# Products on x times the norm's weights for the first token group: one decoder step on one core

## The chip, the core and the metric

The kernel runs on one core of one Trainium2 chip. The metric is the device time of one execution in microseconds (us); 2378.42 is the median of three runs of the kernel before.

## What is computed

One layer of a hybrid decoder over 1088 tokens (1024 of a prompt, 64 of eight samples), width 1024, in fp32. The change touches only its first stage, the first half-step FFN, with d_ff = 2816:

```python
def rmsnorm(x, g):
    xf = xf * lax.rsqrt(jnp.mean(xf * xf, axis=-1, keepdims=True) + EPS)
    return xf.astype(x.dtype) * g
def swiglu_ffn(x, g, w_gate, w_up, w_down):
    h = rmsnorm(x, g)
    return (jax.nn.silu(h @ w_gate) * (h @ w_up)) @ w_down
x = x + 0.5 * swiglu_ffn(x, p['ffn1_norm'], ...)
```

The root of a token multiplies its whole column, so it can be applied to x or to the product. Token mixing, cross attention, a second FFN and a last norm follow.

## The kernel before, in words

Activations lie as 128 partitions by 8 rows (`KT`, 1024 features) by tokens. The tokens are three groups n = 0, 1, 2 of 384, 384 and 320 (`NS`). Every fp32 product is made of three (`split_mm`, L1782 to L1784): a weight tile and its operand are each split into a high part in fp32r (a copy) and a low part (the rest), and TensorE makes high by high, high by low and low by high.

The FFN runs in 11 iterations (`ITS`) of two of the 22 tiles of d_ff. An iteration has six `gate_up` steps and then 24 down tiles. In iteration 0 the steps go group by group (`ffn_step`): steps 0 and 1 are group 0 with the first and second tile, steps 2 and 3 group 1, steps 4 and 5 group 2. A step is 24 gate products and 24 up products, into PSUM banks 4 and 5 (even steps) or 6 and 7 (odd). Down tile (n, m) is six products into bank m % 4, and from the fifth tile on it waits until VectorE has added an earlier tile into x (`x_added`, L1342).

Each engine works off its own list in order:

- SyncE issues the loads: x for group 0 in two halves of 768 KB, gate and up weights of the first tile (512 KB each), x of group 1, weights, x of group 2, weights, and then `st_raw`.
- ScalarE copies the weights' high parts (`ffn_prep`, L783), squares x (`norm_squares`, L818), takes the root (`norm_root`, L843), copies the high parts of normed rows (`pair_highs`, L858), applies silu (`step`, L869), and copies the high part of the later stages' weights (`stage_prep`, L794).
- GpSimd makes the low parts of weights: `low` (L704) and `stage_low` (L709), in the order in which ScalarE delivers.
- VectorE adds up the squares (`norm_sum`, L1173 and L1174), takes the reciprocal (L1166), scales the rows by weight and root (`pair_scale`, L1244), makes their low part (`pair_low`, L1256), and in `hidden(s)` makes silu times up (`hf`, L1326), its high part (`h_hi`, L1330) and low part (`h_lo`, L1332). After all six `hidden` it adds the down tiles into x.
- TensorE also makes the norm's statistics (`norm_stats`, L1809) and spreads a root over the partitions (`norm_spread`, L1844) into a bank called `rb`. In ffn1 of group 0 all of this stands ahead of the first product: squares, sums, statistics, root, spread, rows, highs, lows.

Pairs of rows (`PAIRED`) are released one by one: a product of rows 2i and 2i + 1 waits for `normed`, the i-th low part.

## Time and profile before

| | |
|---|---|
| median of 3 runs | 2378.42 us (2377.48 to 2379.25) |
| profiled execution | 2381.26 us |
| its span | 2379.5 us |
| TensorE busy | 2345.2 us (99%) |
| VectorE / ScalarE / GpSimd busy | 1065.7 / 500.7 / 519.7 us |
| granted TensorE clock, mean | 0.995 |

The table gives averages over the whole span. TensorE is busy nearly throughout; a query of a stretch of the timeline shows when an engine works and what ended its idle time.

### The profile page before, as it was taken

Reading aid. Unit: us, or ns where it says so; the run is one execution under the profiler, and the core shown is the slowest. Engines: PE = TensorE matmul, PEld = TensorE weight load, DVE = VectorE, ACT = ScalarE, POOL = GpSimd, SP = SyncE. Lnnn points to the kernel's source line nnn. Section 1 sums busy time; section 2 is a strip of 40 time slices with the busy share of each in tenths; the row PEclk is TensorE's granted clock in tenths of the full one; section 3 lists DMA queues with packets and bytes.
Section 4 is the critical chain, followed back from the end, with each engine's and each line's share of the span. In section 5 each row is a group of like instructions: output and inputs, shape, how many; then the busy total and the mean of one; then the engine's idle time right before and its main releaser. Section 6 shows DMA issues by size and latency. Waiting matters only on the chain. (4 is left out here: it accounts for less than half of the span.)

```text
span 2379.5 us, 36667 instructions
## 1 busy us (share of the span) xinstructions
PE 2345.2 (99%) x15002; PEld 2286.1 (96%) x15002; DVE 1065.7 (45%) x1696; ACT 500.7 (21%) x705; POOL 519.7 (22%) x239
## 2 busy tenths in 40 slices
PE   7999999999999999999999999999999999999998
PEld 7999999999999989899889999799999999999998
DVE  6534334444334574565642423445443344443345
ACT  4222212122211241321410211331111111111112
POOL 2444334344432000000001000022221222221121
PEclk9999999999999999999989999999999999999999
DMA  4554444454452465566668476731111011101112
GB/s 158 213 212 167 159 194 174 152 212 167 159 194 89 154 217 181 212 222 240 231 240 327 142 265 237 276 124 54 51 38 52 36 53 35 53 35 53 35 36 76
DMA packets 89475, 352.50 MB, mean 148 GB/s; under 512 B 8944, under 2 KB 16432, under 8 KB 79152
## 3 DMA queue, kind: packets, MB, share of 16 engines
q1 hardware_dynamic: 89104, 351.12, 40.1%
q8 instruction: 64, 1.05, 0.2%
q10 hardware_dynamic: 288, 0.18, 0.0%
q14 instruction: 19, 0.16, 0.0%
HBM read 280.54 MB, written 70.72 MB: 148 GB/s over the span
## 5 line engine op out<-in xcount | busy, mean ns | idle before, releaser
L1782 PE MATMUL ps<-a_hi,w_sb 128*128 128x384 f32 (+1 forms) x2112 | 690.9, 327 | 6.6 <-DVE a_lo L1256 4.5
L1784 PE MATMUL ps<-a_hi,w_sb 128*128 128x384 f32 (+1 forms) x2112 | 689.1, 326 | 0.0
L1783 PE MATMUL ps<-a_lo,w_sb 128*128 128x384 f32 (+1 forms) x2112 | 689.0, 326 | 0.0
L704 POOL TENSOR_TENSOR w_sb<-w_raw,w_sb 128x1024 fp32r<-128x1024 f32 x132 | 318.0, 2418 | 1063.7 <-ACT w_sb L783 1063.7
L1782 PEld LDWEIGHTS ps<-a_hi,w_sb 128*128 128x128 f32 x2112 | 396.9, 188 | 8.4 <-issue 3.6
L1783 PEld LDWEIGHTS ps<-a_lo,w_sb 128*128 128x128 f32 x2112 | 397.0, 188 | 0.0
L1784 PEld LDWEIGHTS ps<-a_hi,w_sb 128*128 128x128 f32 x2112 | 397.0, 188 | 0.0
L1342 DVE SCALAR_TENSOR_TENSOR x<-ps,x 128x384 f32<-128x384 f32 (+1 forms) x528 | 279.2, 534 | 202.2 <-PE ps L1784 202.1
L1326 DVE TENSOR_TENSOR hf<-sil,ps 128x384 f32<-128x384 f32 x132 | 70.2, 532 | 635.3 <-ACT sil L869 635.3
L1782 PE MATMUL ps<-h_hi,w_sb 128*128 128x384 f32 (+1 forms) x1056 | 344.6, 326 | 0.3 <-DVE h_lo L1332 0.2
L1784 PE MATMUL ps<-h_hi,w_sb 128*128 128x384 f32 (+1 forms) x1056 | 344.2, 326 | 0.0
L1783 PE MATMUL ps<-h_lo,w_sb 128*128 128x384 f32 (+1 forms) x1056 | 344.1, 326 | 0.0
L869 ACT ACTIVATE sil<-ps 128x384 f32<-128x384 f32 x132 | 62.6, 474 | 1123.8 <-PE ps L1784 1123.8
L1332 DVE TENSOR_TENSOR h_lo<-hf,h_hi 128x384 fp32r<-128x384 f32 x132 | 241.6, 1830 | 4.6
L1782 PEld LDWEIGHTS ps<-h_hi,w_sb 128*128 128x128 f32 x1056 | 198.2, 188 | 1.0 <-DVE h_lo L1332 0.5
L1783 PEld LDWEIGHTS ps<-h_lo,w_sb 128*128 128x128 f32 x1056 | 198.2, 188 | 0.0
L1784 PEld LDWEIGHTS ps<-h_hi,w_sb 128*128 128x128 f32 x1056 | 198.2, 188 | 0.0
L738 POOL TENSOR_TENSOR sq<-sq 128x768 f32<-128x768 f32 (+2 forms) x17 | 30.0, 1763 | 648.0 <-ACT sq L818 648.0
L783 ACT ACTIVATE w_sb<-w_raw 128x1024 fp32r<-128x1024 f32 x132 | 139.1, 1055 | 98.5 <-DMA w_raw<-in_ffn_gate 90.4
L709 POOL TENSOR_TENSOR st_w<-st_raw,st_w 128x1024 fp32r<-128x1024 f32 x60 | 145.4, 2454 | 48.7 <-ACT st_w L794 48.7
L1782 PE MATMUL ps<-mo_hi,w_sb 128*128 128x384 f32 (+1 forms) x384 | 125.7, 327 | 0.6 <-DVE mo_lo L1726 0.6
L1784 PE MATMUL ps<-mo_hi,w_sb 128*128 128x384 f32 (+1 forms) x384 | 125.1, 326 | 0.0
(266 smaller groups left out, 2731.7 us busy)
## 6 DMA issues: line engine op xcount, KB each, us to landing
w_sb<-split SPq DMA_DIRECT2D x148, 1024.0 KB, 5.3
split<-st_w SPq DMA_DIRECT2D x60, 1024.0 KB, 4.1
st_raw<-in_mix_tiles SPq DMA_DIRECT2D x60, 512.0 KB, 5.8
w_raw<-in_ffn_gate SPq DMA_DIRECT2D x44, 512.0 KB, 3.6
w_raw<-in_ffn_up SPq DMA_DIRECT2D x44, 512.0 KB, 4.4
w_raw<-in_ffn_down SPq DMA_DIRECT2D x44, 512.0 KB, 4.3
kc<-in_cache_k SPq DMA_DIRECT2D x5, 1024.0 KB, 9.2
kc<-in_cache_v SPq DMA_DIRECT2D x4, 1024.0 KB, 9.8
```

Of the source, the lines that this page charges most:

```text
L704: nc.gpsimd.tensor_tensor(w_lo_sb[:, slot_, :], raw[:, slot_, :], w_hi_sb[:, slot_, :].bitcast(F32), ALU.subtract)\
L709: nc.gpsimd.tensor_tensor(st_w[:, j % 3, 1, :], st_raw[:, j % 3, 1, :], st_w[:, j % 3, 0, :].bitcast(F32), ALU.subtract)\
L738: nc.gpsimd.tensor_tensor(buf[:, 0:2, 0:p.N], buf[:, 0:2, 0:p.N], buf[:, 2:4, 0:p.N], ALU.add).then_inc(pool_half, 1)
L783: nc.scalar.activation(w_hi_sb[:, slot_, :], raw[:, slot_, :], ACT.Copy).then_inc(w_hi, 1)
L869: nc.scalar.activation(sil[:, s % 2, 0:N], ps[:, 4 + 2 * (s % 2), 0:N], ACT.Silu).then_inc(silu_done, 1)
L1326: nc.vector.tensor_tensor(hf[:, s % 2, 0:N], sil[:, s % 2, 0:N], ps[:, b + 1, 0:N], ALU.mult).then_inc(h_done, 1)
L1332: nc.vector.tensor_tensor(h_lo[ft][:, tokens(n)], hf[:, s % 2, 0:N], h_hi[ft][:, tokens(n)].bitcast(F32), ALU.subtract)\
L1342: nc.vector.scalar_tensor_tensor(out=x[:, m, tokens(n)], in0=ps[:, LAST_BANKS[m % 4] if last and f and n == 2 else m % 4, 0:NS[n]], scalar ...
L1782: nc.tensor.matmul(dst, w_h, x_h, start=start, stop=False)
L1783: nc.tensor.matmul(dst, w_h, x_l, start=False, stop=False)
L1784: return nc.tensor.matmul(dst, w_l, x_h, start=False, stop=stop)
```

## The change

In iteration 0, the steps 0 and 1 (group 0) no longer wait for the norm. ScalarE copies the high part of x times the norm's weight (`raw_highs`), VectorE makes the low part from x in one operation (`raw_lows`), and TensorE multiplies these. When a step's products are done, VectorE multiplies its two banks by the spread root, in place (`scale_raw`), and silu reads them then. Group 0's normed operands, which iterations 1 to 10 use, are made later, in two halves (`renorm`), ahead of the `hidden` of steps 4 and 5; they pass through `sq` instead of `frow`. The statistics and spreads of groups 0 and 1 now stand between TensorE's products. The first gate tile is loaded between the two halves of x and split in two halves. The norm's 8 weight columns are loaded first, apart from the other constants. The bank of group 0's spread (bank 1) is held until `renorm` is through with it, so down tile (0, 1) waits for its release. The scheme of turns gives group 2's spread bank 2. In ScalarE's list, silu of step 3 moves ahead of the three `stage_prep`.

The diff, with less indentation and without semaphore declarations, the split of the constants' load, and renumbered counts:

```diff
 NORMS = {}
-PAIRED = [("ffn1", 0), ("ffn1", 1), ("ffn1", 2), ("mix", 0), ("ffn2", 1), ("ffn2", 2)]
+PAIRED = [("ffn1", 1), ("ffn1", 2), ("ffn1", 0), ("mix", 0), ("ffn2", 1), ("ffn2", 2)]
 AFTER_XA = [("xan", 1), ("xan", 2), ("ffn2", 0)]
...
     ring = 4
-if key[1] == "fin":
+if key == ("rb", "ffn1", 2, 0):
+    b = 2
+    _next[ring] += 1
+elif key[1] == "fin":
     b = {0: 0, 1: 2, 2: 6}[key[2]] + (key[0] == "rb")
...
+    if (kind, n) == ("ffn1", 0):
+        return sq[:, 2 * i % 4:2 * i % 4 + 2, 0:NS[0]]
     if kind == "mix":
...
     load_x_half(0, x_in[0])
-    load_x_half(1, x_half_in)
...
         sp.wait_ge(stored, 16 * 5)
+    elif k == 1:
+        load_x_half(1, x_half_in)
     elif k in (2, 4):
...
     for k in range(4):
+        if f == 0 and k == 0:
+            for half in range(2):
+                c = slice(512 * half, 512 * half + 512)
+                pool.wait_ge(first_hi, half + 1)
+                ins = nc.gpsimd.tensor_tensor(w_lo_sb[:, 0, c], raw[:, 0, c], w_hi_sb[:, 0, c].bitcast(F32), ALU.subtract)
+                ins.then_inc(w_lo if half else first_lo, 1)
+            continue
         low(k, before + k + 1)
...
-    def pair_highs(kind, n):
+    def pair_highs(kind, n, first=0, last=4):
-        for i in range(4):
+        for i in range(first, last):
             if i < 3:
...
+    def raw_highs(lo, hi):
+        if lo == 0:
+            act.wait_ge(gains_in, 16)
+            act.wait_ge(x_in[0], 16)
+        if lo == 4:
+            act.wait_ge(x_half_in, 16)
+        for r in range(lo, hi):
+            c = GAINS["ffn1"] + r
+            nc.scalar.activation(a_hi[0][:, r, :], x[:, r, tokens(0)], ACT.Copy, scale=vec[:, c:c + 1]).then_inc(raw_hi, 1)
+    def first_weights(half):
+        if half == 0:
+            act.wait_ge(raw_in[0], 16)
+        c = slice(512 * half, 512 * half + 512)
+        ins = nc.scalar.activation(w_hi_sb[:, 0, c], raw[:, 0, c], ACT.Copy).then_inc(first_hi, 1)
+        if half:
+            act.wait_ge(first_hi, 2)
+            nc.scalar.activation(st[:, 0, 1, 8:9], st[:, 0, 0, 0:1], ACT.Copy).then_inc(w_hi, 1)
     def ffn(f):
...
     act.wait_ge(gu_done, f * GATE_UP_STEPS + q0 + s + 1)
+    if f == 0 and first and s < 2:
+        act.wait_ge(raw_scaled, s + 1)
     if f or not first or s >= 2:
...
     if f == 0:
-        norm_squares("ffn1", 0)
-        ffn_prep(0, 0, 0)
+        raw_highs(0, 2)
+        first_weights(0)
+        raw_highs(2, 4)
+        first_weights(1)
+        raw_highs(4, 8)
         ffn_prep(0, 0, 1)
+        norm_squares("ffn1", 0)
+        norm_squares("ffn1", 1, (0,))
+        ffn_prep(0, 0, 2)
         act.wait_ge(const_in, 32)
         norm_root("ffn1", 0)
-        norm_squares("ffn1", 1, (0,))
-        pair_highs("ffn1", 0)
         norm_squares("ffn1", 1, (1,))
+        ffn_prep(0, 0, 3)
     else:
...
         norm_squares("ffn2", 1, (1,))
-    ffn_prep(f, 0, 2)
-    ffn_prep(f, 0, 3)
+        ffn_prep(1, 0, 2)
+        ffn_prep(1, 0, 3)
     norm_root(kinds[0], 1)
...
         pair_highs(kinds[0], 2)
+        if f == 0:
+            step(q0, 3, first)
+            pair_highs("ffn1", 0, 0, 2)
     else:
...
             stage_prep(it, j)
-    step(q0, 3, first)
+    if f or not first:
+        step(q0, 3, first)
     if f and last:
...
     step(q0, 4, first)
+    if first and f == 0:
+        pair_highs("ffn1", 0, 2, 4)
     if not last:
...
+    def raw_lows():
+        dve.wait_ge(gains_in, 16)
+        dve.wait_ge(x_in[0], 16)
+        for r in range(KT):
+            if r == 4:
+                dve.wait_ge(x_half_in, 16)
+            dve.wait_ge(raw_hi, r + 1)
+            c = GAINS["ffn1"] + r
+            nc.vector.scalar_tensor_tensor(out=a_lo[0][:, r, :], in0=x[:, r, tokens(0)], scalar=vec[:, c:c + 1],
+                                           in1=a_hi[0][:, r, :].bitcast(F32), op0=ALU.mult, op1=ALU.subtract).then_inc(raw_lo, 1)
     def norm_pairs(kind, n):
...
+    def scale_raw(s):
+        rb = frow[:, 3, tokens(0)]
+        if s == 0:
+            full_wait(dve, "rb", "ffn1", 0, 0)
+            link(nc.vector.tensor_copy(rb, bank("rb", "ffn1", 0, 0)[:, 0:NS[0]]))
+        dve.wait_ge(gu_done, s + 1)
+        b = 4 + 2 * s
+        for u in range(2):
+            ins = nc.vector.tensor_tensor(ps[:, b + u, 0:NS[0]], ps[:, b + u, 0:NS[0]], rb, ALU.mult)
+        ins.then_inc(raw_scaled, 1)
+    def renorm(lo, hi):
+        for i in range(lo, hi):
+            pair_scale("ffn1", 0, i)
+            if i:
+                pair_low("ffn1", 0, i - 1)
+        if hi == 4:
+            pair_low("ffn1", 0, 3)
     def hidden(s):
...
         if f == 0:
-            norm_head("ffn1", 0)
-            norm_pairs("ffn1", 0)
-        norm_head(kinds[0], 1, (1,) if f else (0, 1))
+            raw_lows()
+            norm_sum("ffn1", 0, 0)
+            norm_sum("ffn1", 0, 1)
+            norm_sum("ffn1", 1, 0)
+            norm_scale("ffn1", 0)
+            norm_sum("ffn1", 1, 1)
+            scale_raw(0)
+            norm_scale("ffn1", 1)
+            pair_scale("ffn1", 1, 0)
+        else:
+            norm_head(kinds[0], 1, (1,))
     if first and s == 1:
-        norm_pairs(kinds[0], 1)
+        if f:
+            norm_pairs(kinds[0], 1)
+        else:
+            for i in range(1, 4):
+                pair_scale("ffn1", 1, i)
+                pair_low("ffn1", 1, i - 1)
+            pair_low("ffn1", 1, 3)
+            scale_raw(1)
         norm_sum(kinds[0], 2, 0)
...
         norm_pairs(kinds[0], 2)
+    if first and f == 0 and s == 4:
+        dve.wait_ge(sq_used, 6)
+        renorm(0, 2)
+    if first and f == 0 and s == 5:
+        renorm(2, 4)
     b = 4 + 2 * (s % 2)
...
     ft, n = ffn_step(grouped, s)
-    if first and s == 0 and f == 0:
-        norm("ffn1", 0)
-    paired = first and ft == 0 and (kinds[0], n) in PAIRED
-    if first and ft == 0 and not paired:
+    unnormed = first and f == 0 and n == 0
+    paired = first and ft == 0 and (kinds[0], n) in PAIRED and not unnormed
+    if first and ft == 0 and not (paired or unnormed):
         pe.wait_ge(normed, NORMS[kinds[0], n].out0 + 2)
-    if n == 0:
+    if n == 0 and not unnormed:
         pe.wait_ge(w_lo, T0 + 6 * it + 2 * ft + 2)
...
         pe.wait_ge(normed, NORMS[kinds[0], n].out0 + k // 2 + 1)
-    if first and s == 1 and u == 0 and k == 4:
+    if unnormed and s == 0 and u == 0:
+        pe.wait_ge(raw_lo, k + 1)
+        if k in (0, 4):
+            pe.wait_ge(w_lo if k else first_lo, 1)
+    elif unnormed and k == 0:
+        pe.wait_ge(w_lo, 2 * ft + u + 1)
+    if unnormed and (s, u, k) == (0, 1, 0):
+        pe.wait_ge(const_in, 32)
+        norm_stats("ffn1", 0, (0,))
+    if unnormed and (s, u, k) == (0, 1, 4):
+        norm_stats("ffn1", 0, (1,))
+    if unnormed and (s, u, k) == (1, 0, 0):
+        norm_stats("ffn1", 1, (0,))
+    if unnormed and (s, u, k) == (1, 0, 2):
+        norm_spread("ffn1", 0)
+    if unnormed and (s, u, k) == (1, 0, 6):
+        norm_stats("ffn1", 1, (1,))
+    if unnormed and (s, u, k) == (1, 1, 2):
+        norm_spread("ffn1", 1)
+    if f and first and s == 1 and u == 0 and k == 4:
         norm_spread(kinds[0], 1)
...
         pe.wait_ge(x_added, X + Q * it + KT * n + m - 3)
+    if first and f == 0 and (n, m) == (0, 1):
+        read_wait(pe, "rb", "ffn1", 0, 0)
     c = slice(m * P, m * P + P)
...
     body(0, True)
+    if f == 0:
+        pe.wait_ge(normed, NORMS["ffn1", 0].out0 + 4)
     with pe.Fori(1, ITS - 1) as it:
```

TensorE's list at the start, before. The a_hi_63 and a_lo_64 are the high and low parts of group 0, cst holds ones and the identity:

```order
L1809 MATMUL ps<-cst,sq 128x1 [waits summed,const_in]
L1809 MATMUL ps<-cst,sq 128x1 x2
L1809 MATMUL ps<-cst,sq_b 128x1 [waits summed]
L1809 MATMUL ps<-cst,sq_b 128x1 x2
L1844 MATMUL ps<-cst,st 128x128 [waits scaled]
L1844 MATMUL ps<-cst,st 128x128 x2
L1782 MATMUL ps<-a_hi_63,w_sb 128x384 [waits normed,w_lo]
```

And now; the first statistic stands behind 24 products:

```order
L1888 MATMUL ps<-a_hi_63,w_sb 128x384 [waits first_lo,raw_lo]
L1889 MATMUL ps<-a_lo_64,w_sb 128x384
L1890 MATMUL ps<-a_hi_63,w_sb 128x384
L1888 MATMUL ps<-a_hi_63,w_sb 128x384 [waits raw_lo]
...
L1915 MATMUL ps<-cst,sq 128x1 [waits summed,const_in,w_lo]
```

Statistics and spread moved from ahead of the products to among them.

VectorE's list from `hidden` of step 3 to the first add into x, before:

```order
L1326 TENSOR_TENSOR hf<-sil,ps 128x384 [waits hid_done,silu_done]
L1330 CAST h_hi_72<-hf 128x384 [waits h_done]
L1332 TENSOR_TENSOR h_lo_73<-hf,h_hi_72 128x384 [waits hhi_done]
L1326 TENSOR_TENSOR hf<-sil,ps 128x320 [waits hid_done,silu_done]
L1330 CAST h_hi_70<-hf 128x320 [waits h_done]
L1332 TENSOR_TENSOR h_lo_71<-hf,h_hi_70 128x320 [waits hhi_done]
L1326 TENSOR_TENSOR hf<-sil,ps 128x320 [waits hid_done,silu_done]
L1330 CAST h_hi_72<-hf 128x320 [waits h_done]
L1332 TENSOR_TENSOR h_lo_73<-hf,h_hi_72 128x320 [waits hhi_done]
L1342 SCALAR_TENSOR_TENSOR x<-ps,x 128x384 [waits down_done] x16
```

And now, from `hidden` of step 4 on (L1297 are scales, L1309 lows):

```order
L1432 TENSOR_TENSOR hf<-sil,ps 128x320 [waits hid_done,silu_done]
L1436 CAST h_hi_70<-hf 128x320 [waits h_done]
L1438 TENSOR_TENSOR h_lo_71<-hf,h_hi_70 128x320 [waits hhi_done]
L1297 SCALAR_TENSOR_TENSOR sq<-x,vec,ps 128x384 [waits normed]
L1297 SCALAR_TENSOR_TENSOR sq<-x,vec,ps 128x384
L1309 TENSOR_TENSOR a_lo_64<-sq,a_hi_63 128x768 [waits hi_out]
L1297 SCALAR_TENSOR_TENSOR sq<-x,vec,ps 128x384 [waits normed]
L1297 SCALAR_TENSOR_TENSOR sq<-x,vec,ps 128x384
L1309 TENSOR_TENSOR a_lo_64<-sq,a_hi_63 128x768 [waits hi_out] x2
L1432 TENSOR_TENSOR hf<-sil,ps 128x320 [waits hid_done,silu_done]
L1436 CAST h_hi_72<-hf 128x320 [waits h_done]
L1438 TENSOR_TENSOR h_lo_73<-hf,h_hi_72 128x320 [waits hhi_done]
```

Four scales and three lows of group 0 have come between the `hidden` of steps 4 and 5, and four scales and one low of it stand ahead of step 4's.

ScalarE's list in the same place, before:

```order
L794 ACTIVATE st_w<-st_raw 128x1024 [waits stage_in0]
L794 ACTIVATE st_w<-st_raw 128x1024 [waits stage_in1]
L794 ACTIVATE st_w<-st_raw 128x1024 [waits stage_in2]
L869 ACT_TABLE_LOAD [waits h_done]
L869 ACTIVATE sil<-ps 128x384 [waits gu_done]
L869 ACTIVATE sil<-ps 128x320 [waits h_done,gu_done]
L783 ACTIVATE w_sb<-w_raw 128x1024 [waits raw_in0]
L783 ACTIVATE w_sb<-w_raw 128x1024 [waits raw_in1]
L869 ACTIVATE sil<-ps 128x320 [waits h_done,gu_done]
```

And now:

```order
L910 ACT_TABLE_LOAD [waits h_done]
L910 ACTIVATE sil<-ps 128x384 [waits gu_done]
L876 ACTIVATE a_hi_63<-sq 128x768 [waits rows_out] x2
L812 ACTIVATE st_w<-st_raw 128x1024 [waits stage_in0]
L812 ACTIVATE st_w<-st_raw 128x1024 [waits stage_in1]
L812 ACTIVATE st_w<-st_raw 128x1024 [waits stage_in2]
L910 ACTIVATE sil<-ps 128x320 [waits h_done,gu_done]
L876 ACTIVATE a_hi_63<-sq 128x768 [waits rows_out]
L876 ACTIVATE a_hi_63<-sq 128x768 [waits bank_free1]
L801 ACTIVATE w_sb<-w_raw 128x1024 [waits raw_in0]
L801 ACTIVATE w_sb<-w_raw 128x1024 [waits raw_in1]
L910 ACTIVATE sil<-ps 128x320 [waits h_done,gu_done]
```

The three stage copies now stand behind silu 3 and two highs that need VectorE's new rows, and ahead of silu 4; two more highs stand ahead of the weight copies and silu 5.

## Rows read from the trace of the kernel before

**Rows 1.** The page: busy time of TensorE, share of the span, instructions.
```profile
PE 2345.2 (99%) x15002; PEld 2286.1 (96%) x15002; DVE 1065.7 (45%) x1696; ACT 500.7 (21%) x705; POOL 519.7 (22%) x239
```

**Rows 2.** Waits of TensorE, whole run: us in total, times, longest.
```profile
PE ps L1809 <- DVE sq L1174: 9.0, 1, 9.0
PE ps L1782 <- DVE a_lo L1256: 4.5, 3, 3.3
...
PE ps L1782 <- POOL w_sb L704: 1.4, 1, 1.4
```

**Rows 3.** Timeline, 0 to 62 us, all engines: start, us, engine, instruction, idle before.
```profile
5.76 1.48 ACT L818 ACTIVATE sq<-x 128x1536 f32<-128x1536 f32 x1 [2.57 <-DMA x<-in_x]
...
7.98 1.48 ACT L818 ACTIVATE sq_b<-x 128x1536 f32<-128x1536 f32 x1 [0.73 <-DMA x<-in_x]
...
10.49 5.07 POOL L704 TENSOR_TENSOR w_sb<-w_raw,w_sb 128x1024 fp32r<-128x1024 f32 x2 [10.04 <-ACT w_sb L783]
...
10.56 1.06 ACT L783 ACTIVATE w_sb<-w_raw 128x1024 fp32r<-128x1024 f32 x1 [0.15 <-DMA w_raw<-in_ffn_up]
...
14.86 2.19 DVE L1244 SCALAR_TENSOR_TENSOR frow<-x,vec,ps 128x384 f32<-128x384 f32 x4 [1.74 <-PE ps L1844]
...
24.46 5.84 POOL L704 TENSOR_TENSOR w_sb<-w_raw,w_sb 128x1024 fp32r<-128x1024 f32 x2 [8.90 <-ACT w_sb L783]
...
25.41 2.65 DVE L1174 TENSOR_TENSOR sq_b<-sq_b 128x384 f32<-128x384 f32 x1
```

**Rows 4.** Timeline of TensorE, 0 to 62 us.
```profile
18.11 0.66 PE L1782 MATMUL ps<-a_hi,w_sb 128*128 128x384 f32 x1 [3.29 <-DVE a_lo L1256]
...
19.20 0.52 PE L1782 MATMUL ps<-a_hi,w_sb 128*128 128x384 f32 x1
19.52 0.52 PE L1783 MATMUL ps<-a_lo,w_sb 128*128 128x384 f32 x1
...
22.73 0.33 PE L1782 MATMUL ps<-a_hi,w_sb 128*128 128x384 f32 x1
22.90 0.33 PE L1783 MATMUL ps<-a_lo,w_sb 128*128 128x384 f32 x1
...
43.65 0.72 PE L1809 MATMUL ps<-cst,sq 128*128 128x1 f32 x6
44.24 0.42 PE L1782 MATMUL ps<-a_hi,w_sb 128*128 128x384 f32 x1
```

**Rows 5.** Timeline, 54 to 78 us, all engines.
```profile
60.67 2.94 ACT L794 ACTIVATE st_w<-st_raw 128x1024 fp32r<-128x1024 f32 x3
...
61.79 7.27 POOL L709 TENSOR_TENSOR st_w<-st_raw,st_w 128x1024 fp32r<-128x1024 f32 x3 [7.60 <-ACT st_w L794]
...
66.37 0.44 ACT L869 ACTIVATE sil<-ps 128x320 f32<-128x320 f32 x1 [0.96 <-PE ps L1784]
...
66.82 2.65 DVE L1332 TENSOR_TENSOR h_lo<-hf,h_hi 128x384 fp32r<-128x384 f32 x1
```

**Rows 6.** Timeline of VectorE, 62 to 110 us.
```profile
74.40 1.98 DVE L1330 CAST h_hi<-hf 128x320 fp32r<-128x320 f32 x1
...
76.82 2.53 DVE L1342 SCALAR_TENSOR_TENSOR x<-ps,x 128x384 f32<-128x384 f32 x5
```

**Rows 7.** Timeline of GpSimd, 62 to 120 us.
```profile
71.44 4.75 POOL L704 TENSOR_TENSOR w_sb<-w_raw,w_sb 128x1024 fp32r<-128x1024 f32 x2 [2.39 <-ACT w_sb L783]
```

**Rows 8.** Timeline of TensorE, 72.5 to 78.5 us.
```profile
73.21 0.34 PE L1782 MATMUL ps<-h_hi,w_sb 128*128 128x384 f32 x1
...
77.42 0.44 PE L1782 MATMUL ps<-h_hi,w_sb 128*128 128x384 f32 x1
```

**Rows 9.** Timeline of VectorE, 0 to 70 us: rows of group 1.
```profile
35.93 0.95 DVE L1256 TENSOR_TENSOR a_lo<-frow,a_hi 128x768 fp32r<-128x768 f32 x1
...
37.97 0.95 DVE L1256 TENSOR_TENSOR a_lo<-frow,a_hi 128x768 fp32r<-128x768 f32 x1
```

**Rows 10.** Timeline of ScalarE, 0 to 62 us.
```profile
40.12 0.85 ACT L858 ACTIVATE a_hi<-frow 128x768 fp32r<-128x768 f32 x1 [1.20 <-DVE frow L1244]
```

More of the change, by code:

```diff
@@ L118 @@
     _norm(*_k)
+for _n, _out in ((1, 0), (2, 4), (0, 8)):
+    NORMS["ffn1", _n].out0 = _out
 TURN = {}
@@ L428, in program @@
         x_half_in, sqrt_ready = sem("x_half_in"), sem("sqrt_ready")
+        gains_in, first_hi, first_lo = sem("gains_in"), sem("first_hi"), sem("first_lo")
+        raw_hi, raw_lo, raw_scaled = sem("raw_hi"), sem("raw_lo"), sem("raw_scaled")
         rows_out, hi_out = sem("rows_out"), sem("hi_out")
@@ L875, in body @@
                         if f == 0:
+                            raw_highs(0, 2)
[3 more added lines that the diff above has]
+                            raw_highs(4, 8)
+                            ffn_prep(0, 0, 1)
                             norm_squares("ffn1", 0)
-                            ffn_prep(0, 0, 0)
-                            ffn_prep(0, 0, 1)
+                            norm_squares("ffn1", 1, (0,))
+                            ffn_prep(0, 0, 2)
                             act.wait_ge(const_in, 32)
                             norm_root("ffn1", 0)
-                            norm_squares("ffn1", 1, (0,))
-                            pair_highs("ffn1", 0)
                             norm_squares("ffn1", 1, (1,))
+                            ffn_prep(0, 0, 3)
                         else:
@@ L946, in ffn @@
                 body(ITS - 1, False, True)
+            act.dma_start(vec[:, 0:8], a["vectors"][:, 0:8]).then_inc(gains_in, 16)
             act.dma_start(cst[:, :], a["consts"][:, 0:NC_A]).then_inc(const_in, 16)
-            act.dma_start(vec[:, 0:NV], a["vectors"]).then_inc(const_in, 16)
+            act.dma_start(vec[:, 8:NV], a["vectors"][:, 8:NV]).then_inc(const_in, 16)
             act.wait_ge(sqrt_ready, 1)
@@ L1887, in gate_up @@
                                 ins.then_inc(gu_done, 1)
-                            if first and s in (0, 2):
+                            if first and (s == 2 or s == 0 and f):
                                 norm_stats(kinds[0], n + 1, (u,))
@@ L2113, in gla_sample_kv @@
                     filled(ins, "kvs", b)
-            pe.wait_ge(const_in, 32)
             ffn(0)
```

## The prediction

> **What bounds the kernel now.** I read the busy times first: TensorE works 2345.2 of 2379.5 us [rows 1], so a change pays only where TensorE stands idle. Next, whom TensorE waited for over the whole run [rows 2]: 9.0 us for the first norm sum and 4.5 us for `a_lo`, both mostly before 62 us; the longest wait after that is 1.4 us. So nothing later can absorb a shift made in iteration 0: what TensorE gains or loses by its end goes to the end of the run. Then the timeline of the start: x's first half is there at 5.76 us, the second at 7.98, the up weights at 10.56 [rows 3], and the first real product starts at 18.11 [rows 4]. That is the target. Last, the tail of iteration 0, where I read VectorE, GpSimd and TensorE side by side [rows 5 to 8]: the first down product is at 73.21, the fifth down tile, which needs VectorE's first add into x, at 77.42, and that add starts at 76.82. This handover has almost no slack, and it is there that I see the cost.
>
> Two prices used throughout. GpSimd's subtraction of 1024 columns takes 2.42 us (7.27 for three) [rows 5]. While one runs, some VectorE work stands still: the sum of 384 that takes 0.56 us elsewhere took 2.65 beside GpSimd's pair of subtractions [rows 3], `h_lo` took 2.65 and ended 0.41 after the third stage subtraction [rows 5], a cast of 320 took 1.98 and ended at 76.38, just after GpSimd did [rows 6, 7]. The scales out of PSUM at 14.86 ran at their normal 0.53 beside a subtraction [rows 3]. So VectorE's casts and its operations on two SBUF tiles wait for a running subtraction, those with a PSUM input don't, and the two engines take turns at the end of each piece.
>
> **The change, part by part.** I lay the new orders on the clock with these durations; times are us from the span's start.
>
> 1. *First product.* The gate weights now follow x's first half. 768 KB took 2.22 us (5.76 to 7.98), so 512 KB take about 1.4: gate at 7.1, x's second half at 9.3, up weights and all later transfers as before, for the bytes ahead of them are the same. ScalarE's half copy ends at 7.8, GpSimd's half subtraction (1.2) at 9.05, TensorE starts at 9.2: 8.9 us earlier.
>
> 2. *Raw products and statistics.* TensorE's first 3.7 us run at 0.32 us a product instead of 0.17 [rows 4], as before. VectorE's eight new `raw_lows` (0.56 each) take turns with GpSimd's two half pieces and, from 12.7 to 15.1, with the up weights; the last is out at 15.6. The two squares' sums come after it (0.96 + 0.56), the first at 17.1. The up products start at 17.8. The two statistics and the spread of group 0, which stood ahead of all products, are now inside the stream at 0.59 each (43.65 to 44.24) [rows 4]: 1.8 us. ScalarE's square of group 1 now waits for that first statistic (`sq` is reused): 18.0 to 19.5, then weights 2 to 20.4, GpSimd to 23.4. TensorE waits for these, and step 1 begins at 24.1.
>
> 3. *Group 1's rows.* Here the lead goes. VectorE has: one sum (0.96), GpSimd's last weights (2.4), the second sum (0.56) to 27.2; the root's copy out of PSUM (0.55) and two products on the banks (0.56 each) to 28.7; the spread of group 1 at 31.2; two scales, `hf`, cast, `h_lo` to 33.8; two scales and a low to 35.7. TensorE finished step 1 at 34.2 and starts step 2 at 35.9. From there each pair of rows costs VectorE 2.04 us (35.93 to 37.97) [rows 9] against 1.04 for TensorE's six products. Before, the pairs also ran from 35.93 on, but step 2 began at 39.3 (24 products ahead of the statistic at 43.65), so nothing of that showed. The up half of step 2 starts at 43.8, before at 44.24 [rows 4]: lead 0.5. Steps 3 to 5 stay the same: group 2's rows are fed as before. TensorE reaches the down products at 72.9 instead of 73.21.
>
> 4. *The tail.* ScalarE: silu 3, two new `a_hi` copies of group 0 (0.85 each [rows 10]), which need VectorE's rows, to 66.7; only then the three stage copies (2.94 [rows 5]), before at 60.67, and behind them silu 4 at 69.6 instead of 66.37. GpSimd's three stage subtractions start at 67.8 instead of 61.79. VectorE: `hf` of step 4 at 70.0; its cast waits for the second stage piece (72.6), its `h_lo` for the third (75.3), ends 75.8; then the second half of `renorm`: four scales (0.53) and three lows (0.96), the last scale ending at 78.8, the last low at 80.8. That scale frees bank 1, for which down tile 1 now waits: TensorE does tile 0 by 73.9 and stands until 79.0, 5.0 us. ScalarE: the last `a_hi` to 79.8, the two weight copies that precede silu 5 (1.06 each, 0.96 apart) to 81.7, silu 5 to 82.0. VectorE: `hf` 82.5; cast held by the first weight subtraction to 83.5; `h_lo` held by the second to 86.4; first add done 86.9. Tile 4 starts at 87.0 instead of 77.42, after 4.9 us idle.
>
> **Sum**: 9.9 us idle less the 0.3 of lead left (87.0 against 77.4 at tile 4) = +9.6. The profiled execution took 2381.26, so 2390.9 for it; it stood 2.84 above the median of the runs, and the same difference on the median 2378.42 gives **2388.0 us**. The down tiles behind follow the adds as before. The three small loads of constants replace two (one more issue of 0.46 on ScalarE's queue); hidden, since x arrives at 5.76, and if the 8 gains came later the front would slip by the difference.
>
> What has no row: VectorE's operation on x and `a_hi`, both in SBUF, with three inputs; the rows have it only with a PSUM input. Bounds: it goes free beside GpSimd as the scales did (front 0.8 earlier, +8.8), or is held as a two-tile subtraction is (+9.6). I take held, the row nearest in operands. The Trainium skill, page "SBUF — State Buffer", section "Who interferes with whom", says that a VectorE instruction with two SBUF inputs and a GpSimd instruction that reads SBUF block each other fully; by it the sum is +9.6, without it +8.8. A product written back into PSUM has no row either: between 0.53 (the scales) and twice that; four of them, +0 to +2.2, I take 0.56. The turns at the tail depend on 0.3 us: if the cast of step 4 comes before the second stage piece starts, one piece falls out of the chain, -2.4. Together +6 to +12.
>
> **Rivals.**
> - *The clock falls in the new gaps.* Before 18.1 TensorE stood 3.3 us idle and its next 12 products took 0.32 us, which is the lower of two levels. The two gaps of 5 us would each cost 12 x 0.15 = 1.8: +11.4 to +13.2, 2389.8 to 2391.6. Against it: the rows show no fall from full speed, only a start, and the granted clock reads 1.00. The skill's page "TensorE: Matmul & The Clock Gate", Part 1, calls the throttled state the default which activity lifts; by it these gaps are where the clock could drop.
> - *No change.* If GpSimd did not hold VectorE in the new orders, group 1's rows would come 2.4 us earlier and the cast and low of steps 4 and 5 at once; tile 4 then starts about 76.4, -1: 2377.4. The held rows speak against it; only other timing of the pieces could do it.
> - *Faster.* TensorE is ready for step 2 at 34.2 against 39.3: a lead of 5.1. It survives if VectorE delivers group 1's first pair by then and its first add by 72.3, that is, if the sums and scales of part 3 overlap TensorE's steps and step 5's silu isn't behind `renorm`: 2373.3. It decides at the first pair's low: by 34.2 or not. Against it: the orders put `renorm` ahead of `hf` in both last steps.
>
> **Chances.** Forecast 0.55; clock falls 0.26; a milder loss still over 0.2% (both turns fortunate) 0.02; no change 0.11; faster 0.06. A measurement here tells about 0.2% (4.8 us) from nothing. The first three are slower, 0.83; same 0.11; faster 0.06. The range leaves out these last two, 0.17, and takes +5 to +14 with the bounds: 2383.5 to 2392.5.
>
> **What would show it.** First product near 9.2; up products near 17.8; `a_lo` of group 1 feeding step 2 with waits of 1 us a pair; then TensorE idle about 5 us before down tile 1, released by VectorE's last scale of `renorm`, and again before tile 4, released by the first add; every mark behind it 9.6 later. Wrong if tile 1 starts at once, if the cast or `h_lo` of steps 4 and 5 take under 1 us, or if products after a gap take 0.32.

## The result and the profile after

The changed kernel takes **2388.08 us** (median of 5, 2385.67 to 2390.62) against 2378.46 (5, 2377.48 to 2379.72) for the kernel before: ratio 1.0035, 95% interval 1.0024 to 1.0047, that is 9.6 us slower, clear of the spread of the runs. The forecast was 2388.0.

The page of the changed kernel, busy times by engine, which answers to [rows 1]:

```profile
PE 2343.9 (98%) x15002; PEld 2283.6 (96%) x15002; DVE 1079.7 (45%) x1709; ACT 504.6 (21%) x715; POOL 519.1 (22%) x240
```

TensorE's waits up to 110 us (us in total, times, longest), which answer to [rows 2]:

```profile
PE ps L1888 <- POOL w_sb L730: 9.4, 1, 9.4
PE ps L1888 <- DVE sq L1297: 4.4, 1, 4.4
PE ps L1888 <- DVE a_lo L1309: 3.6, 4, 1.5
PE ps L1888 <- DVE x L1448: 2.6, 1, 2.6
```

TensorE's work is the same; what changed is where it stands idle. The 9.0 us for the first norm's sum are gone, the first product now waits for the first weights' low half (L730) until 9.4 us, and two waits are new: 4.4 us for VectorE's last scale of `renorm` (L1297) and 2.6 us for its first addition (L1448). After 110 us the two kernels have the same list of waits, from 2.2 us for the norm's reciprocals down.

TensorE's timeline around these (start, us, line, operation, idle before):

```profile
9.39 0.66 PE L1888 MATMUL ps<-a_hi,w_sb 128*128 128x384 f32 x1 [9.39 <-POOL w_sb L730]
...
36.30 0.41 PE L1888 MATMUL ps<-a_hi,w_sb 128*128 128x384 f32 x1 [1.54 <-DVE a_lo L1309]
...
43.58 0.80 PE L1915 MATMUL ps<-cst,sq 128*128 128x1 f32 x6 [0.91 <-DVE sq L1227]
44.24 0.42 PE L1888 MATMUL ps<-a_hi,w_sb 128*128 128x384 f32 x1
...
73.19 0.34 PE L1888 MATMUL ps<-h_hi,w_sb 128*128 128x384 f32 x1
...
78.80 0.69 PE L1888 MATMUL ps<-h_hi,w_sb 128*128 128x384 f32 x1 [4.38 <-DVE sq L1297]
79.28 0.52 PE L1889 MATMUL ps<-h_lo,w_sb 128*128 128x384 f32 x1
...
86.29 0.44 PE L1888 MATMUL ps<-h_hi,w_sb 128*128 128x384 f32 x1 [2.64 <-DVE x L1448]
```

Three things are to be read here. The first product is 8.7 us earlier than [rows 4] have it. The up half of step 2 begins at 44.24, to the hundredth where it began before [rows 4], so all of the lead is gone by then. And the down products begin at 73.19, again as before [rows 8], but the fifth tile begins at 86.29 instead of 77.42. I use the last addition of the first iteration as the mark for what the first iteration costs: 97.27 us before, 106.11 after, **+8.84**.

The profiled executions differ by less (2386.3 against 2379.5 us of span, 6.8). ScalarE's timeline shows where: the same two instructions in the kernel before and in the changed one, 1100 and 1500 us in, before first, after second.

```profile
1099.11 1.06 ACT L818 ACTIVATE sq<-memx 128x1024 f32<-128x1024 f32 x1 [15.31 <-DVE mo_lo L1230]
...
1502.93 0.26 ACT L843 ACTIVATE st<-ps,vec 128x3 f32<-128x3 f32 x1 [11.96 <-PE ps L1809]
```

```profile
1108.00 1.06 ACT L836 ACTIVATE sq<-memx 128x1024 f32<-128x1024 f32 x1 [15.30 <-DVE mo_lo L1283]
...
1508.83 0.26 ACT L861 ACTIVATE st<-ps,vec 128x3 f32<-128x3 f32 x1 [11.96 <-PE ps L1915]
```

The shift is 8.89 at 1100 us and 5.90 at 1500. In between, from 1140 to 1260 us, the granted clock of the kernel before was 0.97 and 0.92 of full speed in two stretches of 60 us, against 1.00 and 0.94 in the same work of the changed kernel: 60 times 0.05 is the 3.0 us. Nothing here ties that to the change: the five executions of the changed kernel alone lie 5 us apart, at mean clocks from 0.994 to 0.996. The medians, 9.6 apart, are the better measure, and +8.84 is the part that the traces tie to the change.

VectorE through the tail, behind it GpSimd, and ScalarE's silu of step 4, the rows that answer to [rows 5 to 7]:

```profile
64.03 2.18 DVE L1297 SCALAR_TENSOR_TENSOR sq<-x,vec,ps 128x384 f32<-128x384 f32 x4
...
70.81 2.26 DVE L1436 CAST h_hi<-hf 128x320 fp32r<-128x320 f32 x1
73.11 2.54 DVE L1438 TENSOR_TENSOR h_lo<-hf,h_hi 128x320 fp32r<-128x320 f32 x1
75.57 1.13 DVE L1297 SCALAR_TENSOR_TENSOR sq<-x,vec,ps 128x384 f32<-128x384 f32 x2
...
77.60 1.14 DVE L1297 SCALAR_TENSOR_TENSOR sq<-x,vec,ps 128x384 f32<-128x384 f32 x2
78.66 1.95 DVE L1309 TENSOR_TENSOR a_lo<-sq,a_hi 128x768 fp32r<-128x768 f32 x2
...
82.39 0.82 DVE L1436 CAST h_hi<-hf 128x320 fp32r<-128x320 f32 x1
83.24 2.52 DVE L1438 TENSOR_TENSOR h_lo<-hf,h_hi 128x320 fp32r<-128x320 f32 x1
85.69 2.51 DVE L1448 SCALAR_TENSOR_TENSOR x<-ps,x 128x384 f32<-128x384 f32 x5
```

```profile
68.11 7.18 POOL L720 TENSOR_TENSOR st_w<-st_raw,st_w 128x1024 fp32r<-128x1024 f32 x3 [13.95 <-ACT st_w L812]
80.64 4.78 POOL L715 TENSOR_TENSOR w_sb<-w_raw,w_sb 128x1024 fp32r<-128x1024 f32 x2 [5.34 <-ACT w_sb L801]
```

```profile
69.83 0.42 ACT L910 ACTIVATE sil<-ps 128x320 f32<-128x320 f32 x1
```

Between 70.3 and 85.7 us VectorE is idle for 1.3 us. Its rows are of two sorts: the new scales and subtractions of group 0 (L1297, L1309), 5.2 us in this stretch and 3.1 just before it, 8.3 together; and four operations on hidden rows that last 2.26, 2.54, 0.82 and 2.52 us, though they take 0.33 and 0.49 us when GpSimd is quiet (below). The first two end just after the second and third of GpSimd's stage subtractions (68.11 to 75.29), the last two just after its two of the weights (80.64 to 85.42).

### The profile page after: what moved, and what is told of

It reads as the page before. It is cut to its first block and busy times, and to the rows that moved or that the text cites. A ratio compares the mean times of both kernels' runs of the same rounds, so it can differ in the third digit from the quotient of the medians.

```text
span 2386.3 us, 36701 instructions
## 1 busy us (share of the span) xinstructions
PE 2343.9 (98%) x15002; PEld 2283.6 (96%) x15002; DVE 1079.7 (45%) x1709; ACT 504.6 (21%) x715; POOL 519.1 (22%) x240
## 5 line engine op out<-in xcount | busy, mean ns | idle before, releaser
L1448 DVE SCALAR_TENSOR_TENSOR x<-ps,x 128x384 f32<-128x384 f32 (+1 forms) x528 | 279.4, 535 | 201.9 <-PE ps L1890 201.8
```

Of the source, the lines that this page charges most:

```text
L1448: nc.vector.scalar_tensor_tensor(out=x[:, m, tokens(n)], in0=ps[:, LAST_BANKS[m % 4] if last and f and n == 2 else m % 4, 0:NS[n]], scalar ...
```

## The experiments

Two theories after the result. **Both together** (mine): group 0's second rows and GpSimd's holds each fit into the slack ahead of the additions by themselves, and only their sum does not. **Waits that add up**: the wait for bank 1 and the wait for the first addition are each worth their own length. Beside them the three rivals of the prediction: the clock, VectorE's own work alone, and a lead that could have been kept. Each result names the last addition of the first iteration, which serves as the mark (97.27 before, 106.11 after). Kernels that were executed once have one time, and times of one kernel lie some us apart; for them I go by the mark. It is not exact either: the first product of the kernels with the new front starts anywhere from 8.94 to 9.39 us, so differences of the mark under 0.5 us say nothing.

### The wait for bank 1 alone

```diff
-   rb = frow[:, 3, tokens(0)]
-   link(nc.vector.tensor_copy(rb, bank("rb", "ffn1", 0, 0)[:, 0:NS[0]]))
+   rb = roots[:, 0, 0:NS[0]]
+   release(nc.vector.tensor_copy(rb, bank("rb", "ffn1", 0, 0)[:, 0:NS[0]]), "rb", "ffn1", 0, 0)
...
+   root = roots[:, 0, 0:NS[0]] if own else bank("rb", kind, n, 0)[:, 0:p.N]
...
-   if first and f == 0 and (n, m) == (0, 1):
-       read_wait(pe, "rb", "ffn1", 0, 0)
```

> Group 0's root keeps a copy of its own in SBUF, which the four pairs of scales read, so TensorE's second down tile no longer waits for bank 1. One queue (mine): both waits before the down tiles look at the same VectorE queue, which ends with the first addition at 85.7 us; the 4.4 us before the second tile go, the wait before the fifth grows by about as much, the last addition of the first iteration stays at 106 us (106.11 now, 97.27 in the kernel before) and the time at 2387 to 2389. Waits that add up: the 4.4 us are the wait's own price; the last addition comes at 101.7 and the time at about 2384. Clock: if the drop after the first idle time cost anything, that goes too, another 1.4 us.

One execution: 2392.33 us, last addition at 108.06. TensorE's timeline with the root's own copy:

```profile
85.93 0.69 PE L1897 MATMUL ps<-h_hi,w_sb 128*128 128x384 f32 x1 [8.79 <-DVE x L1457]
...
90.58 0.51 PE L1899 MATMUL ps<-h_hi,w_sb 128*128 128x384 f32 x1
90.90 0.36 PE L1897 MATMUL ps<-h_hi,w_sb 128*128 128x384 f32 x1
```

And one stretch of it (us, TensorE's busy time and instructions, granted clock, share and rate of the DMA engines):

```profile
87.00:92.00 5.00, 5.00 (x20) 0.61 0.08 32
```

The wait for bank 1 is gone, and the three tiles it had held run at once; then TensorE stands for 8.79 us until the first addition, which comes at 85.33 instead of 85.69. So the waits do not add up: both look at the same VectorE queue, and removing the first only lengthens the second. My expectation of the mark (106) missed by 2 us all the same, and the clock is why. After 8.79 us of idling the next 15 products start 0.32 us apart, the lower of the two levels [rows 4], and the granted clock from 87 to 92 us is 0.61 of full speed. From the fifth tile to the last addition it now takes 22.13 us instead of 19.82. In the changed kernel the same thing happened a gap earlier, where it did not show: there the ten products from 78.80 on start 0.32 apart, but they are tiles 1 to 3, which had to wait for the first addition anyway. The idle time before the fifth tile is 2.6 us and not the 4.9 forecast mostly because those tiles ran slowly, 1.5 us in all; the rest is the first addition, 0.6 us earlier than forecast.

### The stage copies after step 5

```diff
-   if f == 0 and not last:
+   if f == 0 and not (first or last):
        for j in range(3):
            stage_prep(it, j)
...
    step(q0, 5, first)
+   if f == 0 and first:
+       for j in range(3):
+           stage_prep(it, j)
```

> ScalarE's three stage copies (and with them GpSimd's three subtractions of 7.2 us) move from before the silu of step 4 to after that of step 5, nothing else. Turns (mine): it is GpSimd that holds VectorE, silu 4 comes 3 us earlier, its cast takes 0.3 instead of 2.3 us, h_lo 0.5 instead of 2.5, and all four pairs are ready before the down tiles: no wait before the second, at most 0.5 before the fifth, last addition at 96.5 to 98, time 2377 to 2380. VectorE's own work: the 12.5 us of scales and subtractions are the price wherever GpSimd works: last addition at 103 or later, time 2385 or more.

2379.16 us (11 runs) against 2381.32 for the kernel before on that chip (21 runs), ratio 0.9994, interval 0.9985 to 1.0003: no difference can be told. Last addition at 96.78. The silu of step 4, and VectorE's timeline:

```profile
66.69 0.42 ACT L910 ACTIVATE sil<-ps 128x320 f32<-128x320 f32 x1
```

```profile
67.66 0.33 DVE L1439 CAST h_hi<-hf 128x320 fp32r<-128x320 f32 x1
68.02 0.49 DVE L1441 TENSOR_TENSOR h_lo<-hf,h_hi 128x320 fp32r<-128x320 f32 x1
68.43 1.13 DVE L1300 SCALAR_TENSOR_TENSOR sq<-x,vec,ps 128x384 f32<-128x384 f32 x2
...
75.26 0.33 DVE L1439 CAST h_hi<-hf 128x320 fp32r<-128x320 f32 x1
75.62 0.49 DVE L1441 TENSOR_TENSOR h_lo<-hf,h_hi 128x320 fp32r<-128x320 f32 x1
76.03 1.94 DVE L1451 SCALAR_TENSOR_TENSOR x<-ps,x 128x384 f32<-128x384 f32 x4
```

GpSimd's:

```profile
75.73 7.35 POOL L720 TENSOR_TENSOR st_w<-st_raw,st_w 128x1024 fp32r<-128x1024 f32 x3 [21.88 <-ACT st_w L812]
```

The same scales and subtractions of group 0 are there, at the same durations. What has shrunk are the cast and `h_lo`: 0.33 and 0.49 us. GpSimd's first piece starts at 75.73, 0.11 after the start of the last `h_lo`, and then only additions with a PSUM input remain, which run at their 0.49 to 0.56 us beside it. All 9 us are back with work put later on other engines. "VectorE's own work is the price" falls; and that work is 8.3 us, not the 12.5 that my expectation says.

Not all of it is GpSimd's, though. The first addition comes at 76.03 instead of 85.69, 9.66 earlier. The four operations on hidden rows are 6.5 us shorter. Another 2.8 come from ScalarE itself: its three copies, 2.93 us, no longer stand ahead of silu 4, which starts at 66.69 instead of 69.83. The last 0.3 is only an earlier start of the whole front. And the edit moves more than three of GpSimd's pieces: its list takes the stage pieces ahead of the two of the weights, so these too leave the tail and start at 83.04 instead of 80.64, behind step 5's `h_lo`.

### The stage copies where the kernel before has them

```diff
    pair_highs(kinds[0], 2)
-   if f == 0:
-       step(q0, 3, first)
-       pair_highs("ffn1", 0, 0, 2)
...
    for j in range(3):
        stage_prep(it, j)
-   if f or not first:
-       step(q0, 3, first)
+   step(q0, 3, first)
+   if f == 0 and first:
+       pair_highs("ffn1", 0, 0, 2)
```

> The stage copies go back ahead of the silu of step 3, where the kernel before has them. Turns: GpSimd's 7.2 us start about 5 us earlier and hold step 3's h_lo and the first pair instead of step 4's; silu 4 no longer waits for the copies, but the queue is the same length: a gain of 1 to 2 us, last addition at 104 to 105.5, time about 2387. Order alone: if it was only silu 4's lateness behind the copies, 3 to 5 us come back, last addition at 101 to 103.

One execution: 2387.55 us, last addition at 106.19, above the 104 to 105.5 that I expected. The queue did get shorter by the 1.5 us that I had expected (first addition at 84.19, not 85.69), but the mark did not move. TensorE again:

```profile
77.30 0.44 PE L1886 MATMUL ps<-h_hi,w_sb 128*128 128x384 f32 x1 [2.91 <-DVE sq L1295]
...
78.18 0.53 PE L1887 MATMUL ps<-h_lo,w_sb 128*128 128x384 f32 x1
78.50 0.53 PE L1888 MATMUL ps<-h_hi,w_sb 128*128 128x384 f32 x1
...
84.80 0.69 PE L1886 MATMUL ps<-h_hi,w_sb 128*128 128x384 f32 x1 [2.53 <-DVE x L1446]
```

After an idle 2.9 us the products run at full spacing until 78.18 and then 0.32 apart, and after the second gap at 84.80 ten do so again (granted clock 0.74 from 79 to 86 us, 0.88 from 86 to 95). The first slow stretch stands in the shadow of the first addition; the second costs 1.6 us from the fifth tile to the last addition (21.39 instead of 19.82), which is what the queue had gained. Here the clock's price is in the open, as it is with the root's own copy. A gain in the queue and a loss in the clock gave a net of nothing, and only the timeline tells them apart.

### The second rows among the additions

```diff
-   if first and f == 0 and s == 4:
-       dve.wait_ge(sq_used, 6)
-       renorm(0, 2)
-   if first and f == 0 and s == 5:
-       renorm(2, 4)
...
+   elif first and f == 0 and n == 0:
+       dve.wait_ge(sq_used, 6)
+       for i in range(4):
+           pair_scale("ffn1", 0, i)
+           if i:
+               pair_low("ffn1", 0, i - 1)
+           add(2 * i)
+           add(2 * i + 1)
+       pair_low("ffn1", 0, 3)
```

> Group 0's second rows, with the root's own copy in SBUF, move from before the hidden rows of steps 4 and 5 to among group 0's additions (a pair of scales, two additions, the previous pair's subtraction), which is the latest place, since the additions change x; GpSimd's stage subtractions stay where they are. Turns (mine): with nothing left of its own to do, VectorE does get step 4's and 5's hidden rows done beside GpSimd, and the rows are then late by what does not fit between the additions: last addition at 99.5 to 101.5, time 2381 to 2383. VectorE's work is the whole price wherever it stands: last addition at 105 or later. All of it hidden: 97.5 or sooner.

One execution: 2380.39 us, last addition at 100.75, inside the range I gave. The edit also holds the root's own copy, and ScalarE's four highs of group 0 move behind silu 5. VectorE's timeline here:

```profile
68.72 2.59 DVE L1441 TENSOR_TENSOR h_lo<-hf,h_hi 128x320 fp32r<-128x320 f32 x1
...
74.13 2.34 DVE L1439 CAST h_hi<-hf 128x320 fp32r<-128x320 f32 x1
...
76.91 1.14 DVE L1302 SCALAR_TENSOR_TENSOR sq<-x,vec,roots 128x384 f32<-128x384 f32 x2
77.97 1.01 DVE L1451 SCALAR_TENSOR_TENSOR x<-ps,x 128x384 f32<-128x384 f32 x2
78.90 1.14 DVE L1302 SCALAR_TENSOR_TENSOR sq<-x,vec,roots 128x384 f32<-128x384 f32 x2
79.95 0.95 DVE L1316 TENSOR_TENSOR a_lo<-sq,a_hi 128x768 fp32r<-128x768 f32 x1
```

GpSimd's holds are still there (cast 1.60 and 2.34, `h_lo` 2.59), and yet the hidden rows of step 5 are done at 76.99. A pair of scales, two additions and a subtraction take about 2.9 us, for two tiles that TensorE makes in 2.08; four such rounds leave TensorE 2.8 us of waiting, in four pieces. Of the 8.84 us, moving the second rows gives back 5.4 and moving GpSimd's pieces 9.3: neither is "the" cost. The two are tied as well: without highs to wait for, ScalarE is at its stage copies sooner, and GpSimd's stage pieces start at 63.30 instead of 68.11. Part of the 5.4 comes that way, and this run does not tell how much.

### Group 0 kept raw

```diff
-   if first and f == 0 and s == 4:
-       dve.wait_ge(sq_used, 6)
-       renorm(0, 2)
-   if first and f == 0 and s == 5:
-       renorm(2, 4)
+   if not first and f == 0 and n in RAW:
+       scale_raw(s, n)
...
-   if f == 0:
-       pe.wait_ge(normed, NORMS["ffn1", 0].out0 + 4)
```

> Group 0 keeps its raw rows all through the first feed-forward: no second rows, and VectorE applies the root to group 0's two product pairs in each of the eleven iterations. Tail is all of it (mine): the first iteration is the kernel before's from 44 us on, no wait before the down tiles above 0.5 us, last addition at 97 to 97.8, and the 1.03 us per step hide behind the next step's 8.3 us of products: time 2378 to 2380, as before. Front keeps its lead: last addition at 92 and 2373. Exposed product: if a step's 1.03 us show in each iteration, 10 us or more, 2388 and above.

2379.35 us (11 runs) against the same 2381.32, ratio 0.9995, interval 0.9986 to 1.0004: no difference. Last addition at 97.31. With GpSimd's holds in place (cast 2.15, `h_lo` 2.58) and no second rows, TensorE has no wait at the down tiles. Its waits up to 110 us, behind the 9.2 us for the first weights:

```profile
PE ps L1874 <- DVE a_lo L1306: 2.8, 3, 1.5
PE ps L1901 <- DVE sq L1224: 1.8, 3, 0.9
```

VectorE's busy time is 1091.8 us, 12 more than with the second rows, since each of the eleven iterations now has four products on group 0's banks, and none of it shows. So the whole tail is the second rows together with the holds, and the front by itself brings nothing that shows: from the up half of step 2 on TensorE waits as in the kernel before. (Here too ScalarE's stage copies, and so GpSimd's pieces, come some 4.7 us earlier than in the changed kernel, since no highs stand ahead of them.)

### A control: the kernel before with late stage copies

The edit of "The stage copies after step 5", made to the kernel before.

> The kernel before, with the three stage copies of the first iteration after the silu of step 5: a control. Mine: the stage work stood in nobody's way there, so nothing moves: last addition at 97.0 to 97.6 (97.27), time as before. If moving the stage copies is worth something by itself: last addition at 96.5 or sooner; if the stage stores then hold up iteration 1's loads: first products of iteration 1 wait, time over 2380.

One execution: 2377.33 us, last addition at 97.05. Where nothing needs their place, moving the stage copies changes the mark by 0.2 us, less than it wanders by itself; the 9.3 us are not a gain of their own. TensorE has no wait from 95 to 300 us, so nothing in the second iteration suffers from the later stage transfers.

### Groups 0 and 1 raw, orders as they were

```diff
-   norm_sum("ffn1", 1, 0)
-   norm_scale("ffn1", 0)
-   norm_sum("ffn1", 1, 1)
+   raw_lows(1, 0, 4)
+   norm_sum("ffn1", 1, 0)
+   norm_scale("ffn1", 0)
+   norm_sum("ffn1", 1, 1)
+   raw_lows(1, 4, 8)
    scale_raw(0, 0)
...
-   for i in range(1, 4):
-       pair_scale("ffn1", 1, i)
-       pair_low("ffn1", 1, i - 1)
-   pair_low("ffn1", 1, 3)
    scale_raw(1, 0)
```

> Groups 0 and 1 keep raw rows; nothing else is put in another order. It asks whether group 1's rows are what gives the front's lead back. Rows are the bound (mine, as in the third step of my prediction): without pairs of scales and subtractions the up product of step 2 starts at 40 to 41 instead of 44.2 us. But the roots and sums, still queued ahead of step 0's and step 2's scaling, are next: step 4 starts only 0.5 to 2 us earlier than the 59 us of the kernel with group 0 alone raw, and the last addition comes at 97 to 98.5. Rows were the only bound: last addition at 92, time 2373.

One execution: 2381.17 us, last addition at 98.31. TensorE's waits after the first 9.0 us:

```profile
PE ps L1905 <- DVE sq L1227: 5.0, 3, 2.4
PE ps L1878 <- DVE x L1438: 1.5, 1, 1.5
PE ps L1878 <- DVE a_lo L1309: 0.3, 1, 0.3
```

The waits of 1.5, 0.7 and 0.7 us for group 1's rows have gone, and step 2's up products begin at 39.76, a lead of 4.5 us: group 1's rows were the bound there. The lead does not last. Of the 5.0 us for sums of squares (L1227), 2.6 fall before step 2; the third wait, 2.44 us until 46.63, stands ahead of step 3 and takes half of the lead. The clock takes most of the rest: behind that wait ten products, from 47.83 on, start 0.32 us apart (granted clock 0.66 from 47 to 52 us), 1.6 us, and here TensorE's own work is the path. Step 4 starts at 58.03, against 58.09 with group 0 alone raw; I had expected a gain of 0.5 to 2 us. At the tail the first addition is held until 77.88, which costs 1.5 us more.

### Groups 0 and 1 raw, orders made for it

```diff
    step(q0, 1, first, it)
+   if f == 0:
+       norm_root(kinds[0], 1)
    norm_squares(kinds[0], 2, (1,))
...
+   if f == 0:
+       norm_scale("ffn1", 1)
+   norm_sum(kinds[0], 2, 1)
    if f == 0:
        scale_raw(2, 1)
-   norm_head(kinds[0], 2, (1,))
+   norm_scale(kinds[0], 2)
...
    step(q0, 3, first, it)
+   ffn_prep(f, it, 5)
...
    step(q0, 5, first, it)
+   if f == 0 and first:
+       for j in range(3):
+           stage_prep(it, j)
```

The edits of the run before are in it too. Of group 1's statistics the first goes later in step 1 and the second, with the spread, into step 2, and its second quad of squares goes into the rows of `frow` that nothing else uses until then.

> Groups 0 and 1 keep raw rows, and the queues are put in order for it: group 1's root after step 1's silu, its statistics and spread in step 2, group 2's second sum ahead of step 2's scaling, the second down weight after step 3, the stage copies after step 5. Mine: the lead of the first product is kept from here on: step 2's up product at 38 to 39 us, step 4 from 52.5, last addition at 91 to 92.5, 5 us ahead of the kernel before, time 2372 to 2374.5. Given back later: if the loads of the second iteration's weights cannot start before the stage's transfers are done, its first products wait, and the time is 2376 or more although the last addition is early.

**2375.16 us** (11 runs, 2373.08 to 2377.26) against 2379.67 (15 runs) for the kernel before on the same chip: ratio 0.9979, interval 0.9970 to 0.9988. It is 4.5 us faster than the kernel before; the changed kernel, 9.6 slower than that one, was not run on this chip. Last addition at 93.01, 4.3 us ahead of the kernel before; I had expected 91 to 92.5, and a time of 2372 to 2374.5. TensorE's waits in the first iteration, all but the first 8.9 us:

```profile
PE ps L1917 <- DVE sq L1236: 1.8, 1, 1.8
PE ps L1890 <- POOL w_sb L716: 1.5, 1, 1.5
PE ps L1890 <- DVE a_lo L1318: 0.6, 1, 0.6
```

No wait stands at the down tiles, and after 95 us the trace shows none up to 300, so the second iteration's loads are in time. Step 2's up products begin at 39.14 and step 4 at 54.05, where I had said 38 to 39 and 52.5. Two waits are left in the front, 1.8 us for the first sum and 1.5 us for GpSimd's third weight, both before 24 us; what they are worth no run shows.

## Why the prediction came out right

Where the time is lost, and through which queue, was forecast rightly. How the loss is made up was not, and the sum held only because the clock's fall, put at nothing, lay where it cost nothing: that is luck. Point by point, by its own steps.

- **First product, raw products.** 9.39 us against 9.2; the last raw low out at 15.53 against 15.6; up products at 17.80 and step 1 at 24.11, as forecast. The operation that had no row, three inputs with two SBUF tiles, is held like a subtraction of two tiles: five of its eight instances take 0.61 us, and the other three 1.22, 1.63 and 2.80, one under each of GpSimd's three pieces (from 7.98, 9.51 and 12.71 on). "Held, +9.6" was the right bound of the two. The Trainium skill, page "SBUF — State Buffer", section "Who interferes with whom", says of two SBUF inputs beside a GpSimd read that the two contend, and the trace agrees with its 2.80 us.
- **A product written back to PSUM** takes 0.56 us (median of four 557 ns), the value taken.
- **Group 1's rows.** Step 2 starts at 36.30, not 35.9, with waits of 1.54, 0.67 and 0.72 us for `a_lo` and then 0.91 for a sum, where I had 1 us a pair. Before, step 2 began at 39.49 (24 products of 0.173 ahead of 43.65), not at 39.3. The up half starts at 44.24: the lead is nil and not 0.5, so the term of -0.3 in the sum should have been 0 (that 0.5 had become 0.3 by the down products was given no reason either). Group 2's first sum, which VectorE now takes after the products on step 1's banks, was not in my reckoning.
- **The tail.** Silu 4 at 69.83 (69.6), step 4's `h_lo` out at 75.65 (75.8), last scale at 78.74 (78.8), silu 5 at 81.42 to 81.83 (82.0), first addition at 85.69 (86.3). Each is within 0.6 us. The fifth tile waits for the first addition alone, so it is at 86.29 and not 87.0: +8.87 there, where the sum had +9.6.
- **What the sum was made of.** I had 9.9 us of idle time less 0.3. The trace has 7.0 us of idle time (4.38 and 2.64), no lead, and 1.5 us of slow products between the two waits. (The remaining 0.3 is in how idle time is counted, from the end of a product that lasts 0.34 us though the next could start after 0.17.) The second wait was mis-sized, 4.9 for 2.6, and the clock was put at nothing; for the most part this is the same stretch of time under two names, since TensorE had to wait for the first addition in any case, standing or slow. So there are not two costs, as 5.0 + 4.9 suggests. There is one: the VectorE queue up to the first addition.
- **The median** agrees better than the working deserves: +8.84 in the trace, +9.6 between medians that move by 2 us with the clock. That 2388.08 lies 0.1 from the forecast is chance.
- **The clock rival** is where the text was wrong. It argued that the rows showed no fall from full speed. The changed kernel's do: products 0.32 us apart from 78.80 to 81.84, granted clock 0.79 from 79 to 86 us. "Products after a gap take 0.32" was one of my own signs of being wrong, and it came. The time came out as forecast because tiles 1 to 3 stood in the shadow of the first addition. Where there was no shadow the price appeared: 2.3 us with the root's own copy, 1.6 with the stage copies first, 1.6 with groups 0 and 1 raw. The Trainium skill's page "TensorE: Matmul & The Clock Gate", Part 1, says that throttling is the default and activity lifts it; it was the better guide than the absence of a row, and I had given it 0.26. I should have asked of each gap whether the products behind it are on the path. Of the rival's two times 1.8 us, the first was there (1.5 measured) but hidden, and the second gap found the clock still up.
- **Faster, no change.** Of the lead of 5.1, 4.3 could be had, with group 1's rows raw and three queues reordered (93.01 against 97.27). The no-change rival asked that GpSimd not hold VectorE; the edit that sees to that at the tail gives 2379.16, no difference from before, where the rival had -1. It is not a pure test of it, since 2.8 us of that came from ScalarE's copies.

What stays open: I did not run the front with the second rows hidden and group 1's rows normed but earlier, so whether the raw rows of group 1 are needed for the gain, or the order alone, isn't shown. The last kernel has the late stage copies and several new orders at once, and their shares are not separated. Nor does anything here say when the clock falls: the same waits were followed by a fall in some kernels and not in others (below).

## What to carry to other kernels

When a change adds work to a queue that feeds a handover, list what else is in that queue at that time, including the time it stands still for its neighbour; here 8.3 us of new VectorE work were free or cost 9 us depending on where three copies of ScalarE, and the GpSimd pieces behind them, stood, none of which had anything to do with it. A start that is 9 us earlier is worth nothing until each later step can start earlier too: follow the lead step by step to the first queue that cannot. And a wait that ends with another engine's event has to be removed at that engine: taking away the first of two waits on one queue gave 4.4 us back and lengthened the second by 6.2.

## What the runs showed of the hardware

- A wait can cost more than its length. After 8.79 us of idling TensorE's next 15 products were 0.32 us apart instead of 0.173, 2.3 us beyond the wait; after 4.38 us ten were.
- The length of the wait does not tell whether it happens. After 2.53 us (stage copies first, 84.80) ten products were slow at once; after 2.64 us in the changed kernel none were. After 2.91 us (stage copies first) the first four had nearly full spacing and the fall came at 78.18, while TensorE was busy. The same two waits at step 2, 1.54 and 0.67 us, were followed by about ten slow products in three kernels (stage copies after step 5, second rows among the additions, group 0 kept raw; granted clock 0.72 from 36 to 42 us) and by none in three others (the changed kernel, the root's own copy, stage copies first; 1.00). There the fall cost nothing, because the waits behind it shrank.
- VectorE's operation on two SBUF tiles and a column of weights took 0.61 us by itself and up to 2.80 beside a GpSimd subtraction; additions with a PSUM input kept their 0.49 to 0.56 us beside one.
- An execution's time follows its mean granted clock: the 11 runs of the last kernel span 2371.3 to 2375.5 us at clocks from 0.997 down to 0.995, and the profiled runs before and after differ by 3 us in the middle stages at granted clocks of 0.97 and 0.92 against 1.00 and 0.94.
